# One core, a two-block transformer step: first-stage sums and low parts on GpSimd, the gate product in four column groups, and head 0 in its own order

## What is computed

```python
h = rms_norm(x, norm_pre)                       # x * rsqrt(mean(x*x) + eps) * norm_pre
(aq, ak, av, az, dq, dk, dv, db, da, dz, gate_att, gate_dn) = split_cols(h @ w_in)
q = apply_rope(rms_norm(heads(aq), q_norm), cos, sin)      # 8 attention heads, 2 of k and v
qkv = silu(short_conv(concat([dq, dk, dv]), conv_w))       # the delta rule's q, k, v
qd, kd = l2_norm(cq) * DN_DK ** -0.5, l2_norm(ck)          # per head, 8 heads
g = -exp(a_log) * softplus(da + dt_bias)                   # decay, 16 columns
beta = sigmoid(db)                                         # 16 columns
o_dn = bidir_gated_deltanet(qd, kd, vd, g, beta)           # g is summed up in chunks of 64 tokens
```

## Time and profile before

| | before |
|---|---|
| median of three runs | 2148.97 us |
| lowest and highest | 2147.11, 2150.16 us |
| the profiled execution | 2146.21 us |
| its span | 2144.4 us |
| PE busy | 2102.0 us (98%) |
| DVE, ACT, POOL busy | 1259.1, 1063.9, 236.8 us |

### The profile page before, as it was taken

One profiled execution on the slowest core, in us unless ns is written; L12 is line 12 of the kernel. 1 busy time (PEld: TensorE's weight loads), 2 busy tenths in 40 slices (PEclk: granted clock), 3 DMA queues, 4 the chain that ended last, 5 costly groups with the idle time before them and its releaser, 6 DMA issues.

```text
span 2144.4 us, 36021 instructions
## 1 busy us (share of the span) xinstructions
PE 2102.0 (98%) x15046; PEld 1681.0 (78%) x15046; DVE 1259.1 (59%) x2218; ACT 1063.9 (50%) x2094; POOL 236.8 (11%) x240
## 2 busy tenths in 40 slices
PE   8999999999999999999999999999999999999999
PEld 6777877877778887877777888888777777888887
DVE  6777767766745456655567443444577775443442
ACT  6667666676665236656665331333455554322331
POOL 1223312221310011100001000000100001000000
PEclk9999999999999999999999999999999999999999
DMA  4321212221224332111112322222211212232222
GB/s 182 109 81 66 90 51 85 85 66 55 71 85 155 124 137 86 59 60 59 60 59 70 111 99 90 87 99 98 84 64 64 65 60 98 98 105 92 98 101 77
DMA packets 36227, 186.89 MB, mean 87 GB/s; under 512 B 4560, under 2 KB 4944, under 8 KB 16992
## 3 DMA queue, kind: packets, MB, share of 16 engines
q1 hardware_dynamic: 36064, 184.58, 25.0%
HBM read 173.00 MB, written 7.90 MB: 84 GB/s over the span
## 4 chain that ended last, share of the span: by engine, by line
PE 89%; DVE 5%; ACT 3%; issue 1%; DMA 1%; SPq 0%; POOL 0%; DVEq 0%; ACTq 0%
PE ps L1879 87%; PE ps L1882 1%; ACT arena L2832 1%; DVE spl L2337 1%; ACT spl L2835 1%; ACT hh L2832 0%; DVE x L2697 0%; DMA raw<-wstream 0%; DVE arena L2356 0%; DVE arena L2640 0%; DVE x L2626 0%; DVE arena L2622 0%; DVE hl L2648 0%; DMA arena<-spill 0%; ACT pad L2832 0%
## 5 line engine op out<-in xcount | busy, mean ns | idle before, releaser
L1879 PE MATMUL ps<-hh,spl 128*128 128x512 f32 (+1 forms) x3152 | 1020.2, 397 | 10.5 <-ACT x L2835 2.2
L1879 PEld LDWEIGHTS ps<-hh,spl 128*128 128x128 f32 x3152 | 585.5, 189 | 144.2 <-issue 17.3
L1879 PE MATMUL ps<-hl,spl 128*128 128x512 f32 (+1 forms) x1568 | 616.3, 393 | 0.0
L2337 DVE TENSOR_TENSOR spl<-raw,spl 128x512 fp32r<-128x512 f32 x596 | 422.1, 732 | 168.8 <-ACT spl L2835 167.9
L1879 PE MATMUL ps<-arena_r,spl 128*128 128x512 f32 x1968 | 468.2, 393 | 10.4 <-DVE arena_r L2349 8.5
L1879 PEld LDWEIGHTS ps<-arena_r,spl 128*128 128x128 f32 x1968 | 371.8, 189 | 89.7 <-issue 10.9
L2835 ACT ACTIVATE spl<-raw 128x512 fp32r<-128x512 f32 x596 | 345.2, 619 | 143.4 <-PE ps L1879 138.2
L1879 PEld LDWEIGHTS ps<-hl,spl 128*128 128x128 f32 x1568 | 295.9, 189 | 60.0 <-issue 4.6
L1879 PE MATMUL ps<-arena 32*32 32x32 f32 (+5 forms) x5664 | 216.6, 225 | 8.2 <-issue 8.0
L2832 ACT ACTIVATE arena<-arena 128x512 f32<-128x512 f32 (+3 forms) x204 | 132.3, 650 | 184.7 <-DVE arena L2702 141.1
L1879 PEld LDWEIGHTS ps<-arena 32*32 32x32 f32 (+4 forms) x5664 | 126.6, 116 | 82.3 <-issue 69.5
(11 more groups left out here) (272 smaller groups left out, 2151.1 us busy)
## 6 DMA issues: line engine op xcount, KB each, us to landing
raw<-wstream SPq DMA_DIRECT2D x148, 1024.0 KB, 4.9
arena<-spill SPq DMA_DIRECT2D x17, 256.0 KB, 5.2
GS<-g_rows SPq DMA_DIRECT2D x16, 256.0 KB, 3.5
spill<-x SPq DMA_DIRECT2D x14, 256.0 KB, 2.0
arena<-arena SPq DMA_DIRECT2D x18, 128.0 KB, 2.0
x<-xT SPq DMA_DIRECT2D x4, 512.0 KB, 6.3
spill<-arena SPq DMA_DIRECT2D x8, 256.0 KB, 2.0
x<-xT SPq DMA_DIRECT2D x1, 2048.0 KB, 7.4
```

What stands on the lines that cost most here:

```text
L1879: return pe.matmul(out, lhsT, rhs, start=start, stop=stop, skip_group_check=True)
L2337: tt(spl[:, p % 2, 1, c], raw[:, p % 2, c], spl[:, p % 2, 0, c].bitcast(F32), ALU.subtract) \
```

## The change

Five things are changed in the first stage, and one in the stream of head 0.

1. The seven adds of `norm_sq` and the eight `h_low` go from DVE to POOL.
2. The first loads: the eight columns of norm_pre come alone (`ld_pre`, 4 KB) ahead of the first weights; the rest of `vec` and the first constants come behind the x and weight pieces. The waits for `ld_vec` move from the top of the engines' programs to the steps that use them. `h_set` (small constants) moves ahead of `tok` and multiplies the gate weights by norm_pre instead of splitting them.
3. `gate_mm` is eight plain float32 matmuls of X[k] with 32 weight columns, the k-th on column group k % 4 of the array, so the four groups hold partial sums; DVE scales all 128 rows, and `gate_tr` becomes four float32 matmuls that turn and sum the groups at once. `gate_cum` has three matmuls in place of nine.
4. Head 0 has its own order, FIRST_STREAM, without dn_z: dn_q, dn_k, att_z, dn_v, att_q. Its dn_q is made from u, not from h; so its result is multiplied by h_rs as it leaves PSUM, by DVE (`cv_in`) in place of ACT.
5. The attention's k0 and k1 enter the rotation after the last `h_x`, not after the third.
6. The planner's costs follow, and with them the order in all eight heads; from the end of the head stage on the order of every engine is as before.

```diff
+FIRST_STREAM = ("dn_q", "dn_k", "att_z", "dn_v", "att_q", "early")
 HEAD_STREAM = ("dn_z", "dn_q", "att_q", "att_z", "dn_v", "dn_k", "early")
...
-                o.main("norm_sq", k, cost=[("AC", AC_B), ("DV", DV_B)])
+                o.main("norm_sq", k, cost=[("AC", AC_B), ("PO", PO_B)])
...
+    o.main("h_set", cost=[("DV", 1.9)])
...
-        if k in (2, 3):
-            o.now = o.at["ar_k", f"k{k - 2}"].t
-            rope_in(f"k{k - 2}", k_uses[k - 2])
-        if k == 2:
-            o.main("h_set", cost=[("DV", 1.2)])
+        if k in (7, 8):
+            o.now = o.at["ar_k", f"k{k - 7}"].t
+            rope_in(f"k{k - 7}", k_uses[k - 7])
...
-            st = o.main("h_low", k - 1, cost=[("DV", DV_B)], after=o.at["h_x", k - 1].t)
+            st = o.main("h_low", k - 1, cost=[("PO", PO_B)], after=o.at["h_x", k - 1].t)
...
-    o.main("gate_mm", cost=[("PE", 5.6), ("DV", 0.7)], u=u)
+    o.main("gate_mm", cost=[("PE", 2.0), ("DV", 0.7)], u=u)
...
-        for what in HEAD_STREAM:
+        for what in HEAD_STREAM if hd else FIRST_STREAM:
             if what in ("dn_k", "dn_q", "dn_v"):
                 o.until(pads.ready)
-                gemm(h, KT, conv_done({"dn_q": 0, "dn_k": 8, "dn_v": 16}[what] + hd))
+                first = hd == 0 and what == FIRST_STREAM[0]
+                gemm(raw_h if first else h, KT, conv_done({"dn_q": 0, "dn_k": 8, "dn_v": 16}[what] + hd, first))
...
             for i in range(4):
                 c = slice(512 * i, 512 * i + 512)
                 sp.dma_start(x[:, 2 * i:2 * i + 2, :], xT[:, 2 * i:2 * i + 2, :]).then_inc(sem(f"ld_x{i}"), 16)
+                if i == 0:
+                    sp.dma_start(vec[:, 0:8], vecs[:, 0:8]).then_inc(sem("ld_pre"), 16)
                 sp.dma_start(raw[:, 0, c], wstream[0][:, c]).then_inc(sem(f"ld_x{i}"), 16)
-                if i == 0:
-                    sp.dma_start(vec[:, :], vecs).then_inc(sem("ld_vec"), 16)
-                    sp.dma_start(cst[:, 0:2, :], consts[:, 0:2, :]).then_inc(sem("ld_vec"), 16)
+            sp.dma_start(cst[:, 0:2, :], consts[:, 0:2, :]).then_inc(sem("ld_vec"), 16)
             sp.dma_start(raw[:, 1, :], wstream[1]).then_inc(sem("ld_w1"), 16)
+            sp.dma_start(vec[:, 8:], vecs[:, 8:]).then_inc(sem("ld_vec"), 16)
             sp.dma_start(wb_raw, wba).then_inc(sem("ld_rest"), 16)
             sp.dma_start(cst[:, 2:, :], consts[:, 2:, :]).then_inc(sem("ld_rest"), 16)
...
                 elif kind == "gate_mm":
-                    w.wait_ge(sem("setup"), 7)
+                    w.wait_ge(sem("setup"), 6)
                     if q.u.n > 1:
                         w.wait_ge(drained[q.u.b], q.u.n - 1)
-                    o = psum[q.u.b][0:32, :]
                     for k in range(KT):
-                        wh, wl = wb_hi[:, k * 32:k * 32 + 32], wb_lo[:, k * 32:k * 32 + 32]
-                        mm(o, wh, HI["u_h"][k], k == 0, False)
-                        mm(o, wl, HI["u_h"][k], False, False)
-                        i = mm(o, wh, HI["u_l"][k], False, k == 7)
+                        i = mm(psum[q.u.b][Q32[k % 4], :], wb_norm[:, k * 32:k * 32 + 32], X[k], k < 4, k > 3)
                     i.then_inc(filled[q.u.b], 1)
                 elif kind == "gate_tr":
                     t = at["gate_mm",].u
                     w.wait_ge(drained[t.b], t.n)
                     if q.u.n > 1:
                         w.wait_ge(drained[q.u.b], q.u.n - 1)
-                    rows = A(40)[0:32, :]
                     for tb in range(4):
-                        i = pe.transpose(psum[q.u.b][:, tb * 32:tb * 32 + 32], rows[:, tb * 128:tb * 128 + 128],
-                                         C["ident"][0:32, 0:32])
+                        i = mm(psum[q.u.b][:, tb * 32:tb * 32 + 32], A(40)[:, tb * 128:tb * 128 + 128],
+                               C["lev4i"][:, 64:96], tb == 0, tb == 3)
                     i.then_inc(filled[q.u.b], 1)
                 elif kind == "gate_cum":
                     w.wait_ge(sem("gate_raw"), 1)
                     b = psum[q.u.b]
                     cum = b[:, 0:64].rearrange("p (t n) -> p t n", t=4)
-                    for tb in range(4):
-                        mm(cum[:, tb, 0:8], C["tri_u"], g3(graw)[:, tb, 0:8], tb == 0, False)
-                        mm(cum[:, tb, 8:16], C["tri_l"], g3(graw)[:, tb, 8:16], False, False)
+                    mm(cum[:, :, 0:8], C["tri_u"], g3(graw)[:, :, 0:8], True, False)
+                    mm(cum[:, :, 8:16], C["tri_l"], g3(graw)[:, :, 8:16], False, False)
                     mm(b[:, 128:192], C["ones"], graw, False, True).then_inc(filled[q.u.b], 1)
...
-                elif kind == "norm_sq":
-                    k = q.key[0]
-                    if k:
-                        w.wait_ge(sem("norm_sq"), k + 1)
-                        if k > 1:
-                            w.wait_ge(sem("norm_add"), k - 1)
-                        tt(sq_acc, sq_acc, sq_tmp[k % 4], ALU.add).then_inc(sem("norm_add"), 1)
...
-                elif kind == "h_low":
-                    k = q.key[0]
-                    w.wait_ge(sem("h_hi"), k + 1)
-                    tt(hl[:, k, :], h_tmp[k % 2], hh[:, k, :].bitcast(F32), ALU.subtract).then_inc(sem("h_lo"), 1)
...
-                    dve.tensor_copy(wb_hi, wb_raw).then_inc(sem("setup"), 1)
+                    tt(wb_norm.rearrange("p (k n) -> p k n", k=KT), wb_raw.rearrange("p (k n) -> p k n", k=KT),
+                       V("norm_pre", 0, KT).unsqueeze(2).to_broadcast([128, KT, 32]), ALU.mult).then_inc(sem("setup"), 1)
...
-                    tt(A(40)[0:32, :], psum[q.u.b][0:32, :], h_rs[0:32, :], ALU.mult).then_inc(drained[q.u.b], 1)
+                    tt(A(40), psum[q.u.b][:, :], h_rs, ALU.mult).then_inc(drained[q.u.b], 1)
...
+                elif kind == "cv_in" and q.raw:
+                    full(q.u)
+                    w.wait_ge(sem("norm_rs"), 1)
+                    tt(pad_of[q.ip], psum[q.u.b][:, :], h_rs, ALU.mult).then_inc(drained[q.u.b], 1)
...
-                if kind == "ar_rot":
+                if kind == "norm_sq" and q.key[0]:
+                    k = q.key[0]
+                    w.wait_ge(sem("norm_sq"), k + 1)
+                    if k > 1:
+                        w.wait_ge(sem("norm_add"), k - 1)
+                    tt(sq_acc, sq_acc, sq_tmp[k % 4], ALU.add).then_inc(sem("norm_add"), 1)
+                elif kind == "h_low":
+                    k = q.key[0]
+                    w.wait_ge(sem("h_hi"), k + 1)
+                    tt(hl[:, k, :], h_tmp[k % 2], hh[:, k, :].bitcast(F32), ALU.subtract).then_inc(sem("h_lo"), 1)
+                elif kind == "ar_rot":
+                    w.wait_ge(sem("ld_vec"), 32)
+                    w.wait_ge(sem("ld_rest"), 48)
                     done, t_ = at["ar_dma", q.key[0]].done, tmp_of.get(q.key[0], ar_tmp)[0]
                     w.wait_ge(sem(done[0]), done[1])
```

More of the change, by code:

```diff
@@ L458, in arrange @@
         if 2 <= k <= 5:
-            o.main("norm_sq", k + 2, cost=[("AC", AC_B), ("DV", DV_B)])
+            o.main("norm_sq", k + 2, cost=[("AC", AC_B), ("PO", PO_B)])
     for u, key in zip(us, ("k0", "k1")):
@@ L478, in arrange @@
                 un = ring.take()
-                t = o.main("norm", cost=[("PE", 0.9), ("AC", 1.3)], u=un).t
+                t = o.main("norm", cost=[("PE", 0.46), ("AC", 1.3)], after=o.at["norm_sq", 7].t, u=un).t
                 ring.give(un)
@@ L535, in decay_lane @@
         u = obank_att.take()
-        o.add("gate_cum", cost=[("PE", 2.2), ("DV", 0.6), ("AC", 0.5)], u=u)
+        o.add("gate_cum", cost=[("PE", 0.8), ("DV", 0.6), ("AC", 0.5)], u=u)
         obank_att.give(u)
@@ L615, in z_done, with conv_done @@
         return done
-    def conv_done(i):
+    def conv_done(i, raw=False):
         def done(u):
             ip, old = pads.take()
-            st = o.main("cv_in", i, cost=[("AC", AC_B)])
-            st.u, st.ip, st.old = u, ip, old
+            st = o.main("cv_in", i, cost=[("DV" if raw else "AC", AC_B)])
+            st.u, st.ip, st.old, st.raw = u, ip, old, raw
             main.give(u)
@@ L1882, in tr @@
                 return pe.transpose(out, in_, C["ident"])
-            w.wait_ge(sem("ld_vec"), 32)
             for q in steps:
@@ L2366, in vector @@
                 elif kind == "h_set":
+                    w.wait_ge(sem("ld_vec"), 32)
+                    dve.tensor_copy(ones_r[:, :], C["ones"])
                     ts(qw, V("q_norm"), 128.0 ** -0.5, None, ALU.mult).then_inc(sem("setup"), 1)
                     w.wait_ge(sem("ld_rest"), 48)
-                    dve.tensor_copy(wb_hi, wb_raw).then_inc(sem("setup"), 1)
+                    tt(wb_norm.rearrange("p (k n) -> p k n", k=KT), wb_raw.rearrange("p (k n) -> p k n", k=KT),
+                       V("norm_pre", 0, KT).unsqueeze(2).to_broadcast([128, KT, 32]), ALU.mult).then_inc(sem("setup"), 1)
                     for n in CR:
@@ L2907, in scalar @@
                     k = q.key[0]
```

(4 more changed lines are left out.)

9 lines of the change are left out of this document (2 added, 7 removed).

## The result

| | before | after |
|---|---|---|
| median (6 runs each) | 2149.56 us | 2157.02 us |
| lowest and highest | 2146.55, 2151.60 | 2153.75, 2158.67 |
| ratio, 95% interval | | 1.0041 [1.0027, 1.0055] |
| profiled execution, span | 2146.21, 2144.4 | 2156.87, 2155.1 |

A forecast was written before the change was run, and what follows sets the result against it. PE, busy 2102.0 of 2144.4 us, was taken to set the end; first stage -2.0 and order of heads -4.0 sum to -6.0, so 2143.0 us against a median of 2148.97, range 2137.5 to 2151.

The forecast's parts named there:

- Start of PE: First loads: PE starts near 7.9 us instead of 8.54, worth nothing by itself because tok waits for w_lo.
- Adds in turns: First stage: POOL's adds and DVE alternate in turns of 1.7 us, so tok starts near 24.8, +2.0 us.
- Low clock behind the gap: First stage: PE's longer wait before tok lowers the granted clock, +1.5 us, between 0 and +2.4.
- Gate product: First stage: sixteen float32 records on four column groups take 2.05 us, -3.4 us; other end +1.4.
- gate_cum: First stage: from eighteen records to six, -1.3 us.
- no wait for `hl`: First product of head 0: PE's 1.30 us wait for tile 7 goes, covered by dn_q from u, -1.3 us.
- gate_tr: First stage: from four records in 0.43 us to eight, +0.5 us.
- First stage: Sum of the terms for tok, clock, gate product, gate_tr, gate_cum and the wait for hl: -2.0 us.
- Heads: Replanned order of the eight heads: fewer large POOL instructions in the level chains, -4.0 us, between -7 and +4.
- The two named level chains: Heads 3 and 5: windows near 9.5 of 10 us PE busy at full clock, losing some 0.8 us each.
- rival 2: Heads gain nothing: level-chain waits move and do not go; -2.0 us alone, 2147.0 us, chance 0.28.
- Rival 3: Level chains of heads 0 to 2: extra waits of 4.0 us each make it slower; two give 2155.0 us, chance 0.10.

The follow-up runs named there:

- x3: The changed kernel with the 4 KB load of norm_pre moved behind the first piece of weights; ratio to before 1.0061.
- w3: The changed kernel with 30 filler instructions at the top of PE and nothing else altered; ratio to before 1.0029.
- y4: The changed kernel with its seven adds on DVE again and 30 filler instructions at the top of PE; ratio to before 1.0015.
- z2: Before's order of heads with the new gate work, loads and dn_q from u, adds and low parts on DVE; ratio to before 1.0044.
- z4: z2 with 96 filler instructions at the top of PE; ratio to before 1.0025.
- x4: The changed kernel with the seven adds on DVE again, low parts still on POOL; ratio to before 1.0041.
- w1: z3 with DVE's scaling of the gate product moved ahead of h_x of tile 6; ratio to before 1.0000.
- v1: w1 with the low part of k0's squares also moved, behind h_x of tile 3; ratio to before 1.0005.
- x2: The changed kernel's order on all engines with the instructions and loads of before; ratio to before 1.0010.
- y1: Before's order with the changed kernel's new instructions, plus 30 filler instructions at the top of PE; ratio to before 1.0032.
- z3: z2 with 32 filler instructions at the top of PE; ratio to before 1.0004.

## Why the prediction was wrong, point by point

- **Start of PE** (7.9): it was 10.36. That it is worth nothing by itself agrees with x3, which started 3.0 sooner and was no faster.
- **Adds in turns** (`tok` +2.0): `tok` was 3.3 later; turns of 1.7 us as worked out, from squares that came 0.6 later, not 1 sooner. Same filler on both sides, F differs by 2.9 (w3, y4). Right mechanism, a third too small.
- **Low clock behind the gap** (+1.5): not there; the clock fell later, behind `gate_tr`'s wait (0.83 in 50:60). Right size at a place not named, by luck; up to the load of `pT` both kernels lose 3.4 us by it, so it is no part of the difference.
- **Gate product** (-3.4 said, -3.5 measured), **`gate_cum`** (0.78 us) and **no wait for `hl`**: right.
- **`gate_tr`** (+0.5): its eight records were, but the wait in front of it, 2.55 us, was missed. The prediction asked what stands behind the moved adds on POOL, not when DVE comes to the scaling of the gate product: it stands at the end of DVE's first stage, here behind ACT's rotation of k0 too, in z2 to z4 without it.
- **First stage** (-2.0): F is +2.2, and with its 1.7 us of low clock +3.9. Without the adds it is -1.4 (x4), where the terms without adds and clock give -5.5. The sum took every term as PE's own, but DVE ends the stage (w1, v1), and PE had no such 5.5 us to win.
- **Heads** (-4.0): this step failed, and it is the larger miss. They cost +9.1 in the profiled executions (W 5.3, S 3.8), +7.4 with the one low-clock stretch less that they have. The two named level chains did fill up, as the prediction had it; the waits went elsewhere and grew (W +5.3), where rival 2 had them unchanged. The step counted large POOL instructions inside the level chains and gave no price to what the new order puts in front of the long products: the new waits are for a DVE instruction at 97.30 (2.41) and for ACT's copies out of PSUM at 282.38, 335.98 and 469.75 (4.7 together). x2 has the loss without the other parts (W +4.1). That two of the losses it read in the earlier trace rows were not data waits was missed too: of the 1.4 us in 340:350, 0.89 at 341.65 and 0.54 at 346.39 are stalls at block borders (numbers 7361, 7618), and no order of lanes takes them away. The 2.33 us at 484.36 are a data wait: all twelve kernels with before's order have it, whatever the count (2.30 to 2.34), and its instruction waits at a semaphore.
- **What no step had**: the count of PE instructions. The change takes some away (23 by the end), every later border lies elsewhere in the bursts, and S goes from 3.6 to 7.3.
- **Rival 3** came nearest (2155.0), but by luck: its two waits of 4 us in heads 0 to 2 are not what the trace shows; there is 2.41 us at 97.30, a data wait, and three stalls of 1.05, 1.21 and 2.18.

What stays open: why most borders cost nothing and a few 2 us. Nearly all stalls came when the block before had been used up in 2.5 to 5 us, but three of four such borders cost nothing. The place within the block can be foretold; which border costs something, and how much, could not (y1, w3). Open too is why the mean clock costs 2 to 6 us more in most kernels that have the new gate work, and how much of a difference between two kernels it makes by chance.

## What to carry to other kernels

Before a change of some tenths of a per cent is credited or blamed, run it with 30, 60 and 100 instructions of dead filler on the engine that bounds: here filler alone moved the time by up to 0.4% (z2, z3), as much as the whole change. Look in the timeline for stops in the middle of a burst without a wait, and number the instructions. And where a first stage is bound by DVE, what is taken off PE comes back as a wait for DVE at its next step.

## What the runs showed of the hardware

- PE stops in front of instruction 193 or 194 of a block of 256 and nowhere else without a wait (118 of 118). Bursts of 64 records, 128 instructions with the weight loads, take 0.74 us and use up a block fastest; 107 of the 118 stops are in front of such a record.
- Four column groups with float32 and 512 columns run side by side: 16 records in 1.92 us, where 16 on the whole array would take 6.9 by the earlier trace rows.
- POOL and DVE on two-input instructions of 128x512 take strict turns: 9.85 us for six on POOL, 6.84 for four on DVE.
- 32x32 float32 matmuls one after another on one tile of the array start 54 ns apart (6.17 us for 112), those of the level chains, spread over the array's tiles, some 9 ns (64 in 0.74 us, the last of them 0.18 long).
